# Rotated key columns of the second block's projection: the 32 weight columns as the stationary operand, tokens as the moving one

## The reference, cut to what matters

```python
p = h @ w_in[l]
pc = hc @ w_in[l]
cq = _rms(p[..., OFF_Q:OFF_KV], q_a_g)          # 384 columns
ckv = _rms(p[..., OFF_KV:OFF_KPE], kv_a_g)      # 256 columns
k_pe = p[..., OFF_KPE:OFF_F]                    # 32 columns: the rotated part of the keys
four_lat = _fourier(p[..., OFF_F:OFF_GA])       # 512 columns
ga = jax.nn.sigmoid(p[..., OFF_GA:OFF_GB])      # 1024 columns
gb = jax.nn.sigmoid(p[..., OFF_GB:N_IN])        # 1024 columns
```

## The kernel before, in words

| groups | job | mode | result |
|---|---|---|---|
| 0 to 5 | cq, 384 columns | T | `lat` |
| 6 to 11 | ckv, 256 columns, latent and context | T | `lat` |
| 12 to 21 | k_pe, 32 columns, ten tiles of 128 tokens | N | `kpe` |
| 22 to 29 | Fourier columns, 512 | T | `fT` |
| 30 to 61 | gates, 2048 columns | T | `go`, then to memory |

## Time and profile before

### The profile page before, as it was taken

The page is one execution under the profiler, slowest core; times in us unless marked ns, Lnnn a source line. Parts: engine busy times, 40 slices in busy tenths (PEclk is TensorE's granted clock), DMA queues, the critical chain, the costliest instruction groups (busy, mean ns, idle before and its releaser), DMA issues. The chain is left out here.

```text
span 3207.7 us, 40595 instructions
## 1 busy us (share of the span) xinstructions
PE 2821.6 (88%) x16494; PEld 2303.7 (72%) x16494; DVE 1521.3 (47%) x2191; ACT 1072.6 (33%) x1886; POOL 329.1 (10%) x322
## 2 busy tenths in 40 slices
PE   5999988999898998993887999988899989929997
PEld 3777767777678787882775888855788867817786
DVE  3225533433545214226635131023666654579997
ACT  4114311111214305223226212112566531207775
POOL 0004400000100000000000000000311010102441
PEclk9999999999999998996998979999999999959999
DMA  6554651221302201106423203221000045239997
GB/s 171 187 189 124 192 167 42 68 75 41 120 23 60 60 25 53 43 22 179 157 87 111 61 13 92 66 85 48 1 1 1 1 150 159 99 126 332 380 374 271
DMA packets 272229, 357.44 MB, mean 111 GB/s; under 512 B 54987, under 2 KB 185059, under 8 KB 270380
## 3 DMA queue, kind: packets, MB, share of 16 engines
q1 hardware_dynamic: 228332, 212.06, 20.7%
q0 software_dynamic: 32192, 121.81, 11.6%
q10 hardware_dynamic: 11520, 20.98, 1.8%
HBM read 282.70 MB, written 76.80 MB: 112 GB/s over the span
## 5 line engine op out<-in xcount | busy, mean ns | idle before, releaser
L225 PE MATMUL ps<-h_hi,st_w_lo 128*128 128x512 f32 x592 | 249.2, 421 | 15.9 <-PEq L834 10.1
L222 DVE TENSOR_TENSOR w_lo<-wraw,w_hi 128x1024 fp32r<-128x1024 f32 (+2 forms) x116 | 120.1, 1053 | 279.1 <-ACT w_hi L219 278.4
L227 PE MATMUL ps<-h_hi,st_w_hi 128*128 128x512 f32 x592 | 235.0, 397 | 0.0
L226 PE MATMUL ps<-h_lo,st_w_hi 128*128 128x512 f32 x592 | 233.6, 395 | 0.0
L222 DVE TENSOR_TENSOR ew_lo<-wraw,ew_hi 128x1024 fp32r<-128x1024 f32 x192 | 223.0, 1218 | 8.5 <-ACT ew_hi L219 7.6
L219 ACT ACTIVATE w_hi<-wraw 128x1024 fp32r<-128x1024 f32 (+2 forms) x116 | 104.1, 916 | 286.0 <-PE ps L227 154.4
L219 ACT ACTIVATE ew_hi<-wraw 128x1024 fp32r<-128x1024 f32 x192 | 190.9, 1056 | 17.7 <-DMA wraw<-w_e_gate 7.0
L225 PE MATMUL ps<-w_hi,merged_lo 128*128 128x512 f32 (+2 forms) x408 | 161.3, 395 | 32.7 <-DVE w_lo L222 30.6
L225 PE MATMUL ps<-h_hi,w_lo 128*128 128x512 f32 x384 | 157.0, 409 | 19.1 <-DVE w_lo L222 19.1
L225 PE MATMUL ps<-merged_hi,w_lo 128*128 128x512 f32 x400 | 160.4, 401 | 9.8 <-DVE w_lo L222 9.8
L226 PE MATMUL ps<-merged_lo,w_hi 128*128 128x512 f32 x400 | 159.7, 399 | 0.0
(11 more groups left out here) (501 smaller groups left out, 6513.8 us busy)
## 6 DMA issues: line engine op xcount, KB each, us to landing
wraw<-w_in SPq DMA_DIRECT2D x98, 512.0 KB, 4.6
wraw<-w_e_gate SPq DMA_DIRECT2D x64, 512.0 KB, 12.1
wraw<-w_e_up SPq DMA_DIRECT2D x64, 512.0 KB, 11.7
wraw<-w_e_down SPq DMA_DIRECT2D x64, 512.0 KB, 12.9
mod_w<-w_mod POOLq DMA_DIRECT2D x12, 2048.0 KB, 9.5
gates<-st_zo ACTq DMA_DIRECT2D x48, 256.0 KB, 2.0
rw_in<-rw_scan POOLq DMA_DIRECT2D x8, 1280.0 KB, 6.1
mg_gates<-gates POOLq DMA_DIRECT2D x16, 512.0 KB, 4.8
```

The source lines that it names most:

```text
L222: return dve.tensor_tensor(dst, src, hi.bitcast(F32), ALU.subtract)
L225: pe.matmul(out, a[1], b[0], start=first, stop=False)
L226: pe.matmul(out, a[0], b[1], start=False, stop=False)
L227: return pe.matmul(out, a[0], b[0], start=False, stop=last)
```

## The change

The k_pe job turns from mode "N" to mode "T". Its 32 weight columns stand in the array, and the 1280 tokens move in slices of 512, 512 and 256. The ten groups become three (12 to 14), the Fourier groups become 15 to 22 and the gates 23 to 54. The result `kpeT` has the 32 channels on partitions. Ten PE transposes turn it back behind group 24, the second gate group (`rope_tokens`), into bank 5, and one ACT copy (`rope_out`) writes `kpe`. Sums 0 moves behind group 14, the last of the k_pe job, and sums 1 behind group 19. The squares for sums 0 are made behind group 12, those for sums 1 behind group 17, in the Fourier job. `pieces_of` now takes widths under 128 in mode "T", and the PSUM slice is as high as the piece is wide.

```diff
@@ -172,7 +172,7 @@
 
         kt, cols = w.shape[1], w.shape[2]
         if mode == "T":
-            return [(w[:, :, m * P:(m + 1) * P], kt, P) for m in range(cols // P)]
+            return [(w[:, :, m:min(m + P, cols)], kt, min(P, cols - m)) for m in range(0, cols, P)]
         per = min(kt, SPLIT // cols)
         return [(w[:, k:min(k + per, kt), :], min(per, kt - k), cols) for k in range(0, kt, per)]
 
@@ -343,7 +343,7 @@
                             first, last = k == uses[0][2], k == uses[-1][2]
                             if job["mode"] == "T":
                                 a = job["act"](k, x)
-                                mm = products(pe, ps[:, n % banks, 0:a[0].shape[-1]], w, a, first, last)
+                                mm = products(pe, ps[0:cols, n % banks, 0:a[0].shape[-1]], w, a, first, last)
                             else:
                                 mm = products(pe, ps[:, n % banks, 0:cols], job["act"](k, m), w, first, last)
                         mm.then_inc(S("gemm_mm"), 1)
@@ -2129,19 +2129,37 @@
 
                 sq = sb(st, "cn_sq", [P, 3, T])
                 rs = sb(st, "cn_rs", [P, NKEY])
+                kpeT = sb(st, "kpeT", [ROPE, NKEY])
                 link = [None]
                 NORMS = ((cq, 3, [(0, 512), (512, 512)], gv[:, 0:3], QL),
                          (ckv, 2, [(0, 512), (512, 512), (1024, 256)], gv[:, 3:5], KVL))
                 squared = lambda i: sq[:, :, :].rearrange("p k t -> p (k t)")[
                     :, 0:NORMS[i][1] * NORMS[i][0].shape[2]].rearrange("p (k t) -> p k t", k=NORMS[i][1])
 
-                def cn_squares(act, m, x, done):
-                    if m in (0, 8):
-                        i = m // 8
-                        act.wait_ge(*done)
-                        if i:
-                            act.wait_ge(S("cn_mm"), 1)
-                        act.activation(squared(i), NORMS[i][0][:, :, :], ACT.Square).then_inc(S("cn_sq"), 1)
+                def cn_squares(act, i, done):
+                    act.wait_ge(*done)
+                    if i:
+                        act.wait_ge(S("cn_mm"), 1)
+                    act.activation(squared(i), NORMS[i][0][:, :, :], ACT.Square).then_inc(S("cn_sq"), 1)
+
+                def rope_part(act, m, x, done):
+                    if x == 0:
+                        cn_squares(act, 0, done)
+
+                def beside_fourier(act, m, x, done):
+                    if (m, x) == (1, 0):
+                        cn_squares(act, 1, done)
+
+                def rope_tokens(pe):
+                    pe.wait_ge(S("cn_mean"), 5)
+                    for t in range(NKT):
+                        tr = pe.transpose(ps[:, 5, t * ROPE:(t + 1) * ROPE], kpeT[:, t * P:(t + 1) * P],
+                                          ident[0:ROPE, 0:ROPE])
+                    tr.then_inc(S("kp_tr"), 1)
+
+                def rope_out(act):
+                    act.wait_ge(S("kp_tr"), 1)
+                    act.activation(kpe[:, :, :].rearrange("p t c -> p (t c)"), ps[:, 5, 0:NKT * ROPE], ACT.Copy)
 
                 def cn_sums(pe, i):
                     _b, kt, slices, _g, _w = NORMS[i]
@@ -2179,15 +2197,21 @@
                       dict(w=wcols(w_in2, QL, QL + KVL), mode="T", tiles=3, on="act", evac=put(ckv),
                            act=lambda k, x: (tuple(h[:, k, x * 512:(x + 1) * 512] for h in latent) if x < 2 else
                                              tuple(h[:, k, :] for h in ctxp))),
-                      dict(w=wcols(w_in2, QL + KVL, OFF_F), mode="N", tiles=NKT, on="act",
-                           act=lambda k, m: (tuple(h[:, k, m * P:(m + 1) * P] for h in latent) if m < NT else
-                                             tuple(h[:, k, (m - NT) * P:(m - NT + 1) * P] for h in ctxp)),
-                           act_step=cn_squares,
-                           evac=lambda kind, eng, src, m, x: copy(kind, eng, kpe[:, m, :], src[:, 0:ROPE])),
-                      dict(w=wcols(w_in2, OFF_F, OFF_F + 512), mode="T", act=whole(latent), tiles=2, evac=put(fT)),
+                      dict(w=wcols(w_in2, QL + KVL, OFF_F), mode="T", tiles=3, on="act",
+                           act=lambda k, x: (tuple(h[:, k, x * 512:(x + 1) * 512] for h in latent) if x < 2 else
+                                             tuple(h[:, k, :] for h in ctxp)),
+                           act_step=rope_part,
+                           evac=lambda kind, eng, src, m, x: copy(
+                               kind, eng, kpeT[:, x * 512:min((x + 1) * 512, NKEY)],
+                               src[0:ROPE, 0:min(512, NKEY - x * 512)])),
+                      dict(w=wcols(w_in2, OFF_F, OFF_F + 512), mode="T", act=whole(latent), tiles=2, evac=put(fT),
+                           act_step=beside_fourier),
                       dict(w=wcols(w_in2, OFF_GA, OFF_GA + 2 * D), mode="T", act=whole(latent), tiles=2, evac=gate,
                            on="act", act_step=gate_out)], ring=4, banks=5,
-                     side={"at": {12 + 4: 0, 22 + 3: 1}, "pe": cn_sums, "act": cn_root, "dve": cn_scale})
+                     side={"at": {14: 0, 19: 1, 24: 2},
+                           "pe": lambda pe, i: rope_tokens(pe) if i == 2 else cn_sums(pe, i),
+                           "act": lambda act, i: rope_out(act) if i == 2 else cn_root(act, i),
+                           "dve": lambda dve, i: None if i == 2 else cn_scale(dve, i)})
 
 
             ctx_stack.close()
```

## The result

| | before | changed |
|---|---|---|
| median, us | 3199.65 (4 runs, 3196.38 to 3202.68) | 3171.99 (4 runs, 3169.41 to 3173.89) |
| span of the profiled execution, us | 3207.7 | 3172.1 |

The ratio on record is 0.990, with a 95% interval of 0.9885 to 0.9915: the changed kernel is faster by 27 to 37 us. The two medians of the table alone differ by 27.7 us, at the lower end of that. The forecast was 3169.4 us, in a range from 3162 to 3181. The kernel before has one more run here than when the forecast was made, which is why its median is 3199.65 and not 3202.05.

What follows compares the result with a forecast made beforehand. PE, busy without a gap and partly at half clock, was taken to bound the projection. Savings of 31.10 + 2.65 less 1.10 for transposes gave 32.65 us, so 3202.05 - 32.65 = 3169.4 us, range 3162 to 3181.

Steps and rivals of the forecast that it cites:

- What bounds the stage: Projection: PE is a plain queue of matmuls, never idle, so what it no longer does comes off the time.
- The k_pe job and sums 0: Start of the k_pe job to the first Fourier matmul: 50.33 us becomes 19.23, saving 31.10 us.
- The clock behind the job: Start of the Fourier job: 5.8 us ran at half clock; if the clock never falls, 2.65 us are saved.
- The transposes: Ten PE transposes among the gate groups, 0.11 us each, add 1.10 us to PE's path.
- ACT and DVE: Copies and moved norm work beside the projection's groups: PE waits for neither, so they cost nothing; 18 us slack for piece 9.
- The sum: Whole kernel: 31.10 + 2.65 - 1.10 = 32.65 us saved, giving a timed median of 3169.4 us.
- the fallen clock: Rival, new k_pe job: narrow stationary operand counts as little work, clock falls after 4.9 us; gain 23.1 us, 3179; chance 9%.
- undisturbed timed runs: Rival, old k_pe job: timed runs kept full clock, unlike the profiled one; gain only 11.3 us, 3191; chance 3%.
- new wait: Rival, projection: slack is missing, PE stands still for two DVE chains, 29 us; about 4 us gain, 3198; chance 3%.
- slow float32r: Rival, k_pe job: narrow float32r runs like plain float32, two passes, 51.6 us instead of 14.07; loss 4.9, 3207; chance 2%.

## Why the prediction was right, by its own steps

- **What bounds the stage.** PE was a queue without a gap in the projection, before and after, so what it no longer does there comes off the time. The stage shrank by 33.1 us, the medians by 27.7, 31.4 and 30.7 us in three comparisons.
- **The k_pe job and sums 0.** 14.07 + 5.16 = 19.23 us were forecast, 13.86 + 5.14 = 19.0 measured (18.6 to the start of the first Fourier record).
- **The clock behind the job.** There is no stretch at 0.50 from the job to the end of the projection, as forecast. No row measures the 2.65 us alone. What is left of the stage's 33.1 us after the job, 50.33 - 19.0 = 31.3 saved, and the transposes, 0.93 added, is 2.7.
- **The transposes.** 1.10 us forecast, 0.93 measured, and the closeness is partly luck. I took 0.11 us each, on the ground that the load of 128 columns sets it. It was 0.063 us each and 0.3 us once. The row that I had read it from gives 0.10 each by the same count; the rest of its 0.88 us was the change of form.
- **ACT and DVE.** The slack was there. Piece 9's low part was ready more than 20 us before its first user.
- **The sum.** 32.65 us forecast, 33.1 in the traces. That the median lay 2.6 us above the forecast belongs to no term of the sum that the traces show: the base of 3202.05 and this comparison are a few runs each, and the kernel before gave medians of 3199.65, 3206.26, 3207.17 and 3203.78 us in four comparisons. How near the median came is therefore partly luck; the stage in the traces is the better test.

What the forecast did not separate, the experiments do. Of the 33.1 us of the stage, about 21 come back by the clock alone, with the old form and all its weight loads (128 columns moving: 21.1 us). The remaining 12 us come from fewer matmuls: 240 at 0.11 us give way to 72 that move 512 or 256 columns each. By their windows the job with sums 0 takes 32.0 us with 128 columns moving and 19.0 in the changed kernel, and the transposes take 0.93 back. The order gives nothing with the old form (1.8 us the other way). With the new form it was not tried by itself; PE waits in neither kernel there.

The rivals: the fallen clock (3179 us) is ruled out by the profile after and by the job done three times. The undisturbed timed runs (3191) are ruled out by the medians. The new wait did not happen, since PE waited nowhere in the stage. Nor did the slow float32r: the distance of 0.23 us was the same for 32 and for 128 stationary columns. In the working of the fallen clock, 24 matmuls at 0.21 us are 5.0 us and not 5.2, which changes nothing.

## What to carry to other kernels

When a matmul has one narrow side, let the narrow side stand in the array and the long one move. Here turning the small result back cost PE 0.93 us, while moving 32 columns per weight load of 128 cost 0.11 us each at full clock and 0.21 at half. A PE that is busy all the time can still run at half clock, so read the granted clock beside the busy share, and where a stretch of small matmuls shows 0.50, try it with wider ones, even if the extra columns are thrown away. Compare two versions by the stage in their traces when they differ by a few us: the medians of the same kernel moved by up to 7.5 us from one comparison to the next, the stage of the changed kernel by 0.1 us over three traces.

## What I had not expected of the hardware

- Work that nobody needed made the kernel faster. With 128 columns moving instead of 32, each of the 240 matmuls still cost 0.11 us, and the job with sums 0 fell from 50.3 to 32.0 us, with a clock of 1.00 instead of 0.50 in its k_pe matmuls. With 64 the clock was lost as with 32, and the stage was 281.5 us in both.
- Four float32 matmuls into four sets of 32 PSUM partitions went on side by side, with a pass of 384 columns every 0.32 us. The version takes two passes of plain float32 where the changed kernel takes float32r, and gains 3.6 us only. Slices of equal length, which would fill the idle third, were not tried.
- Loading 128 stationary columns does not cost the same everywhere: 0.11 us from start to start in the float32r matmuls of the k_pe job, 0.063 us in the float32 transposes of 32 rows.
